# Expert gate/up weights read as one run per partition in a DeltaNet, attention and MoE layer

## The reference, cut to what matters

```python
def moe_ffn(x, router_w, router_bias, w_gate_up, w_down, ws_gate_up, ws_down):
    scores = sigmoid(xt @ router_w)                      # 512 x 64
    _, sel = lax.top_k(scores + router_bias, TOP_K)
    ...
    gu = x_pad[tok] @ w_gate_up[e]                       # w_gate_up[e]: 1024 x 512
    h = jax.nn.silu(gu[:, :EXPERT_DIM]) * gu[:, EXPERT_DIM:]
    y = (h @ w_down[e]) * wt[:, None]                    # w_down[e]: 256 x 1024
    ...
x = layer_norm(ALPHA * x + mix, ln1_g[l], ln1_b[l])
x = layer_norm(ALPHA * x + ffn, ln2_g[l], ln2_b[l])
```

## Time and profile before

| | |
|---|---|
| runs of the kernel before, median (lowest, highest) | 1773.01 us (1768.64, 1789.97) |
| the profiled execution: span from first to last instruction | 1775.4 us |
| busy: TensorE, VectorE, ScalarE, GpSimd | 82%, 29%, 18%, 18% |
| mean granted TensorE clock | 0.885 of full speed |
| SyncE's DMA queue | 167040 packets, 268.85 MB |
| GpSimd's DMA queue | 11008 packets, 25.45 MB |
| store of one tile to x1_rows, issue to landing | 2.6 us |
| expert stage, final stage in the trace | about 1070 to 1690 us, 1705 to 1775 us |

### The profile page before, as it was taken

The page is one execution under the profiler, slowest core; times in us unless marked ns, Lnnn a source line. Parts: engine busy times, 40 slices in busy tenths (PEclk is TensorE's granted clock), DMA queues, the critical chain, the costliest instruction groups (busy, mean ns, idle before and its releaser), DMA issues. The chain is left out here.

```text
span 1775.4 us, 21709 instructions
## 1 busy us (share of the span) xinstructions
PE 1455.1 (82%) x7304; PEld 864.8 (49%) x7305; DVE 518.1 (29%) x932; ACT 325.1 (18%) x848; POOL 311.8 (18%) x379
## 2 busy tenths in 40 slices
PE   7999999999998998799996938898869868985900
PEld 5566556655663332588745524454444434443400
DVE  1544444444431233233331831111101101110127
ACT  1231333133221223222201000111101101110100
POOL 1202220221121111100012011122112212221113
PEclk8999999999998887799997859999879978997955
DMA  3611111111000000343404507899999996899653
GB/s 98 179 36 35 35 35 35 33 28 33 0 0 24 24 24 0 84 112 95 159 24 175 210 28 253 293 340 398 396 394 348 397 397 244 306 398 396 234 221 142
DMA packets 178919, 295.93 MB, mean 167 GB/s; under 512 B 11504, under 2 KB 81232, under 8 KB 178880
## 3 DMA queue, kind: packets, MB, share of 16 engines
q1 hardware_dynamic: 167040, 268.85, 42.8%
q0 software_dynamic: 11008, 25.45, 3.8%
q10 hardware_dynamic: 832, 1.11, 0.2%
HBM read 284.86 MB, written 22.83 MB: 173 GB/s over the span
## 5 line engine op out<-in xcount | busy, mean ns | idle before, releaser
L1686 PE MATMUL bank<-expert_gu,gathered_xT 128*64 128x256 f32 x2048 | 254.7, 405 | 47.9 <-DMA expert_gu<-in_expert_w_gate_up_dram 36.2
L402 PE MATMUL bank<-xT,w_head 128*128 128x512 f32 x480 | 239.7, 606 | 0.8 <-PEq L77 0.8
L1686 PEld LDWEIGHTS bank<-expert_gu,gathered_xT 128*64 128x64 f32 x2048 | 161.5, 146 | 129.1 <-DMA expert_gu<-in_expert_w_gate_up_dram 38.1
L1827 DVE SCALAR_TENSOR_TENSOR hidden<-gate,slot_w,bank 128x128 f32<-128x128 f32 x64 | 22.2, 348 | 412.5 <-ACT gate L1798 412.5
L568 POOL TENSOR_TENSOR LO<-LT,masks 128x512 f32<-128x512 f32 x56 | 69.4, 1266 | 372.3 <-DVE LT L723 372.3
L1693 PE MATMUL bank<-expert_down,hiddenT 128*64 128x512 f32 x512 | 125.0, 609 | 0.6 <-issue 0.6
L402 PEld LDWEIGHTS bank<-xT,w_head 128*128 128x128 f32 x480 | 81.2, 197 | 41.6 <-issue 41.6
L1798 ACT ACTIVATE gate<-bank 128x128 f32<-128x128 f32 x64 | 17.8, 279 | 353.3 <-PE bank L1686 353.3
L1615 POOL DMA_INDIRECT y_rows<-expert_y,row_col x64 | 64.4, 1006 | 49.4 <-POOL row_col L1612 47.5
L1134 DVE TENSOR_TENSOR w_lo<-w_tile,w_hi 128x1024 fp32r<-128x1024 f32 (+1 forms) x32 | 36.0, 1127 | 125.3 <-ACT w_hi L1088 125.3
L1612 POOL COPY row_col<-row_idx 128x1 int32 (+1 forms) x64 | 11.7, 183 | 328.2 <-ACT expert_y L1804 327.7
(11 more groups left out here) (353 smaller groups left out, 2259.0 us busy)
## 6 DMA issues: line engine op xcount, KB each, us to landing
expert_gu<-in_expert_w_gate_up_dram SPq DMA_DIRECT2D x64, 2048.0 KB
expert_down<-in_expert_w_down_dram SPq DMA_DIRECT2D x64, 1024.0 KB, 19.9
w_head<-in_w_in_dram SPq DMA_DIRECT2D x32, 512.0 KB, 3.8
choices<-y_rows SPq DMA_DIRECT2D x24, 512.0 KB, 15.1
w_tile<-in_w_in_dram SPq DMA_DIRECT2D x16, 512.0 KB, 4.0
w_tile<-in_w_branch_a_dram SPq DMA_DIRECT2D x8, 512.0 KB, 5.4
w_pair<-in_w_in_dram SPq DMA_DIRECT2D x6, 512.0 KB, 3.8
x_rows<-in_x_dram SPq DMA_DIRECT2D x4, 512.0 KB
```

The costliest lines, as they stand in the source:

```text
L402: mm = nc.tensor.matmul(bank[:, :], w_head[:, g, c, :], xT[:, c, :], start=(c == 0), stop=(c == KC - 1))
L1686: mm = nc.tensor.matmul(bank[parts[a], 0:2 * P], x[:, c, part], halves[:, a, :, :], start=(c == 0), stop=(c == KC - 1))
```

## The change

1. Gate/up weights of an expert: partition p gets model columns 8p to 8p+7, which lie together in DRAM, as one run of 16 KB, instead of eight rows of 2 KB at columns p, 128+p and so on. The router's and the shared expert's gate/up weights are read in the same order (runs of 2 KB and of 16 KB).
2. So that x has the same order, ScalarE writes a permuted copy of each normalised tile (`permute`), and both the store to `x1_rows` and the transposes read it. The copies lie in buffers that the merge no longer uses. SyncE waits for the four stores at the end of the phase.
3. Final stage: eight transfers, each with three choices of a tile (runs of 12 KB). GpSimd adds choices 0 and 1, VectorE adds 2, 3, 4, 5 and then that pair. The bias is added by GpSimd on one half of the columns and by VectorE on the other.

```diff
+    x_cols = [T["av"][:, 2 * t:2 * t + 2, :].rearrange("p a n -> p (a n)") for t in range(2)] + \
+             [w_t[:, KC * t:KC * (t + 1), :].rearrange("p a n -> p (a n)") for t in range(2)]
...
             for t in range(TT):
-                sp.wait_ge(ln_done[t], 1)
-                sp.dma_start(x1_rows[t * P:(t + 1) * P, :], xs[:, t, :]).then_inc(x1_out, 16)
+                sp.wait_ge(permuted[t], 1)
+                sp.dma_start(x1_rows[t * P:(t + 1) * P, :], x_cols[t]).then_inc(x1_out, 16)
+            sp.wait_ge(x1_out, 16 * TT)
...
-                        pe.wait_ge(ln_done[t], 1)
+                        pe.wait_ge(permuted[t], 1)
...
+            def permute(t):
+                act.wait_ge(ln_done[t], 1)
+                nc.scalar.copy(x_cols[t].rearrange("p (c q) -> p c q", c=KC),
+                               xs[:, t, :].rearrange("p (q c) -> p c q", c=KC)).then_inc(permuted[t], 1)
...
                 nc.scalar.activation(mv[:, t, 3:4], mv[:, t, 2:3], ACT.Exp, scale=-0.5).then_inc(ln_rs[t], 1)
+                if t:
+                    permute(t - 1)
+            permute(TT - 1)
...
-            sp.dma_start(wr[:, :, :], router_w.rearrange("(c p) n -> p c n", p=P)).then_inc(r_in, 16)
+            sp.dma_start(wr[:, :, :], router_w.rearrange("(p c) n -> p c n", p=P)).then_inc(r_in, 16)
...
-            sp.dma_start(wg[:, :, :], ws_gu.rearrange("(c p) n -> p c n", p=P)).then_inc(s_in, 16)
+            sp.dma_start(wg[:, :, :], ws_gu.rearrange("(p c) n -> p c n", p=P)).then_inc(s_in, 16)
...
-                for k in (4, 5, 0, 1, 2, 3):
-                    sp.dma_start(yt[:, t, k, :], rows[t, :, k, :]).then_inc(y_in[t][k], 16)
+                for m in range(PARTS):
+                    k = m * TOPK // PARTS
+                    sp.dma_start(yt[:, t, k:k + TOPK // PARTS, :].rearrange("p k c -> p (k c)"),
+                                 rows[t, m, :, :]).then_inc(y_in[t][m], 16)
...
+            def add_bias(t):
+                pool.wait_ge(ln_m[t], 1)
+                at = slice(0, HALF)
+                nc.gpsimd.tensor_tensor(xs[:, t, at], xs[:, t, at], b_row[:, at], ALU.add).then_inc(ln_done[t], 1)
+
             for t in range(TT):
...
+                pool.wait_ge(y_in[t][0], 16)
+                nc.gpsimd.tensor_tensor(yt[:, t, 0, :], yt[:, t, 0, :], yt[:, t, 1, :], ALU.add).then_inc(pair_done[t], 1)
+                if t:
+                    add_bias(t - 1)
+            add_bias(TT - 1)
...
+                dve.wait_ge(ln_m[t], 1)
+                at = slice(HALF, D)
+                nc.vector.tensor_tensor(xs[:, t, at], xs[:, t, at], b_row[:, at], ALU.add).then_inc(ln_done[t], 1)
...
-            part = expert_w_gate_up[0][bass.ds(e, 1)].rearrange("e (c p) n -> p (e c) n", p=P)
+            part = expert_w_gate_up[0][bass.ds(e, 1)].rearrange("e (p c) n -> p (e c n)", p=P)
```

More of the change, by code:

```diff
@@ L987, in merge_phase @@
     x1t_psum, x1t_ready = mem.sem("x1t_psum"), mem.sem("x1t_ready")
+    permuted = mem.sems("permuted", TT)
     xs, xT, dnT, aoT, ident, eps = T["x"], T["xT"], T["dnT"], T["aoT"], T["ident"], T["eps"]
@@ L1005, in merge_phase @@
     TURNS = KC // 2
+    x_cols = [T["av"][:, 2 * t:2 * t + 2, :].rearrange("p a n -> p (a n)") for t in range(2)] +              [w_t[:, KC * t:KC * (t + 1), :].rearrange("p a n -> p (a n)") for t in range(2)]
     def two_on(i, p, k):
@@ L1076, in _ @@
                     if c == 0:
-                        pe.wait_ge(ln_done[t], 1)
+                        pe.wait_ge(permuted[t], 1)
                     if c >= 4:
                         pe.wait_ge(x1t_ready, c - 3)
-                    mm = nc.tensor.transpose(ps[c % 4][:, t * P:(t + 1) * P], xs[:, t, c * P:(c + 1) * P], ident[:, :])
+                    mm = nc.tensor.transpose(ps[c % 4][:, t * P:(t + 1) * P], x_cols[t][:, c * P:(c + 1) * P], ident[:, :])
                 mm.then_inc(x1t_psum, 1)
@@ L1867, in final_phase @@
 def final_phase(nc, mem, T, ps, ln_g, ln_b, y_rows, out):
-    y_in = [mem.sems(f"y_in{t}_", TOPK) for t in range(TT)]
+    PARTS = 2
+    y_in = [mem.sems(f"y_in{t}_", PARTS) for t in range(TT)]
     s_done, pair_done = mem.sems("s_done", TT), mem.sems("pair_done", TT)
@@ L1874, in final_phase @@
     xs, eps = T["x"], T["eps"]
+    HALF = D // 2
     yt = mem.sb("choices", [P, TT, TOPK, D])
@@ L1878, in final_phase @@
     mv = mem.sb("ln2_mv", [P, TT, 4])
-    rows = y_rows.rearrange("(t p k a) c -> t p k (a c)", t=TT, p=P, k=TOPK)
+    rows = y_rows.rearrange("(t p m k a) c -> t m p (k a c)", t=TT, p=P, m=PARTS, k=TOPK // PARTS)
     with nc.Block() as block:
@@ L1885, in _ @@
             for t in range(TT):
-                for k in (4, 5, 0, 1, 2, 3):
-                    sp.dma_start(yt[:, t, k, :], rows[t, :, k, :]).then_inc(y_in[t][k], 16)
+                for m in range(PARTS):
+                    k = m * TOPK // PARTS
+                    sp.dma_start(yt[:, t, k:k + TOPK // PARTS, :].rearrange("p k c -> p (k c)"),
+                                 rows[t, m, :, :]).then_inc(y_in[t][m], 16)
             for t in range(TT):
-                sp.wait_ge(ln_done[t], 1)
+                sp.wait_ge(ln_done[t], 2)
                 sp.dma_start(out[0, t * P:(t + 1) * P, :], xs[:, t, :]).then_inc(out_done[t], 16)
@@ L1906, in _ @@
         def _(pool):
+            def add_bias(t):
+                pool.wait_ge(ln_m[t], 1)
+                at = slice(0, HALF)
+                nc.gpsimd.tensor_tensor(xs[:, t, at], xs[:, t, at], b_row[:, at], ALU.add).then_inc(ln_done[t], 1)
             for t in range(TT):
[L1908 to L1914, removed]
+                pool.wait_ge(y_in[t][0], 16)
[3 more added lines that the diff above has]
+            add_bias(TT - 1)
         @block.vector
         def _(dve):
-            HALF = D // 2
             for t in range(TT):
-                for i, k in enumerate((4, 0, 1, 2, 3)):
-                    dve.wait_ge(*((pair_done[t], 1) if k == 4 else (y_in[t][k], 16)))
+                for i, k in enumerate((2, 3, 4, 5, 0)):
+                    if k == 0:
+                        dve.wait_ge(pair_done[t], 1)
+                    elif k in (2, 3):
+                        dve.wait_ge(y_in[t][k // 3], 16)
                     if i:
@@ L2005, in load_gu @@
         def load_gu(sp, s, e, free=None):
-            part = expert_w_gate_up[0][bass.ds(e, 1)].rearrange("e (c p) n -> p (e c) n", p=P)
+            part = expert_w_gate_up[0][bass.ds(e, 1)].rearrange("e (p c) n -> p (e c n)", p=P)
             if free:
                 free()
-            sp.dma_start(T["wgu"][:, s, :, :], part).then_inc(T["gu_in"][s], 16)
+            sp.dma_start(T["wgu"][:, s, :, :].rearrange("p c n -> p (c n)"), part).then_inc(T["gu_in"][s], 16)
         def load_down(sp, s, e, free=None):
```

## The result

The changed kernel takes 1830.84 us (median of 4 runs, 1827.49 to 1838.57) against 1781.49 us (4 runs, 1768.64 to 1791.19) for the kernel before on the same chip: a ratio of 1.028 [1.0226, 1.0334]. The forecast was 1760 with a range to 1790. The profiled executions span 1831.1 and 1775.4 us.

| profiled execution | to the merge | merge | routing to the first expert product | experts | last stage | span |
|---|---|---|---|---|---|---|
| before | 721.7 | 233.8 | 109.4 | 640.5 | 70.0 | 1775.4 |
| after | 738.9 | 236.1 | 109.7 | 675.1 | 71.4 | 1831.1 |
| after, profiled again | 721.5 | 236.6 | 108.3 | 673.1 | 71.2 | 1810.8 |

What follows compares the result with a forecast made beforehand. Weight transfers were taken to bound 344 us of the expert stage, TensorE and overflow blocks the rest outside, VectorE the last stage. -21 + 5 + 0.6 + 2 = -13 from the 1773.0 us median gave 1760, range 1744 to 1790.

Steps and rivals of the forecast that it cites:

- What longer packets do to the other queue: Expert stage: GpSimd's gathers land 2 us later (bounds 0 and 4.2) behind longer weight packets; 5 us more in all.
- in the full stretches that is free: Expert stage, where DMA is full: later gathers cost nothing, a pair lasting 16.9 us by DMA against 15.2 by the gather.
- Rival B: Expert stage: a gather waits behind a fixed 28 packets, landing after 13.0 us; +44, total 1817, chance 0.09.
- Rival A: Expert stage: each gather packet always waits for a 16 KB one, landing after 11.3 us; +6, total 1779, chance 0.22.
- The weight transfers: Expert stage, full stretches: 16 KB runs make each of 38 gate/up loads 0.55 us shorter; 21 us less (bounds 0 and 33).
- The permutation: Before the experts: ScalarE's last strided copy adds 1.5 us, faster router weight reads give 0.9 back; together +0.6.
- the gain for the router's rows: Router weights read as 2 KB runs instead of 256 B rows: TensorE's bias-row wait 0.9 us less (bounds 0 and 2).
- The last stage: Final adds on VectorE and GpSimd: first tile 3.2 us late, the rest 47.2 instead of 48.6; net +2 (bounds -4 and +6).
- The first meeting: Last stage: VectorE's first add runs beside GpSimd's pair add and takes 3.2 us instead of 1.23, costing 1.95.

Runs made afterwards that it cites:

- e1: The changed kernel with GpSimd issuing a pair's gather before the scatter that stood in front of it: 1765.8 us, ratio 0.989 to the kernel before.
- e12: e1 with a pause before each gather of the loop, GpSimd clearing 4096 columns that nobody reads: 1768.17 us in one execution.
- e2: The kernel before with only the gather issued ahead of the scatter: 1779.28 us, ratio 0.9987 to the kernel before.
- e9: The changed kernel with each scatter cut from 128 rows to 16, the last stage reading the merge's output instead: 1819.89 us in a single execution.
- e4: The changed kernel with each gate/up load cut into four transfers of 4 KB runs: 1772.1 us, ratio 0.9958 to the kernel before.
- e3: The changed kernel with each gate/up load cut into two transfers of 8 KB runs: 1777.07 us, ratio 0.9966 to the kernel before.

## Why the prediction was wrong

**The step that failed** is "What longer packets do to the other queue". It had the place, and bounds of 0 and 4.2 us for what a gather takes longer, and took 2, the middle, for want of a row between the ends. Measured: 5.1 us in the buffer whose landings the trace shows, and about 3.3 in the other (10.4 against 7.1). Without the scatter in front it is 3.0 to 3.3 (10.5 and 10.8 in e1 and e12 against 7.5 in e2), inside the bounds. In the shipped order the scatter has at most 1.1 of it (e9); the bounds left it out. The text also had wrong what an issue waits for: it said the buffer's transposes, but the buffer of the gather issued at 1306.67 was free at 1289.84 already, and the gather stood behind the scatter of 1304.70. From the 2 us followed "in the full stretches that is free", and a term of +5 in the sum, where TensorE's waits for gathers grew by 83.7 us and took the whole gain of the loads with them.

**The threshold made the error large.** The text had the loop: a pair of slots can't be shorter than a gather's landing and the 6.2 us from its transposes to the next issue, so the full stretches stay free up to a landing of 16.9 - 6.2 = 10.7 us. "In the full stretches that is free" should have been read as 1.7 us away from not free. But the 6.2, held fixed, grew too. For the gathers issued from 1268.07 on, up to the issue at 1347.82, the transposes begin 9.9 to 12.5 us after the issue (mean 11.7), and the next issue comes 8.0 to 8.4 us behind them (mean 8.3; 1319.16 to 1327.36 in the timeline above), because the next gather stands behind a scatter that waits for the down products right behind the wait, the slow ones. Together that is 19.9 us a pair, against the 16.9 forecast and 18.0 before. With 8.3 the threshold is at 8.6 us, below the 9 us that the forecast itself gave the gather. The issue-to-need distance in the earlier trace rows, 6.4 us for a gather of 7.0, says it more directly: slack was negative before.

**Rival B** came out by its signs of failure (gathers after 12 us, waits past 40 us). That its number did too (1817 against 1817.4 and 1830.8) is luck: it put 41 us on the expert stage, which grew by 34.6 and 32.6. Its mechanism fails. With runs of 4 KB, 28 packets ahead of 0.16 us each would make 4.3 + 4.5 = 8.8 us, and with 8 KB 10.9; the gather took 7.5 (e4) and 8.5 (e3). The Trainium skill (DMA: Bandwidth & Descriptors, Queues, rings and completion order) has an engine change queues only between packets of some 9 to 17 descriptors. These runs don't decide on it. If a gather's eight rows on an engine are one such packet, they wait once for eight 16 KB runs, an estimated 4.9 us, and that sum is the same as one run in front of each of eight rows. Only eight such waits in a row are excluded, since e1's gather is 3.0 us later in all. Rival A's sum fits best: its 4.2 against 3.0 to 3.3 in e1 and e12, and its 11.3 us for a gather against the 12.2 and 10.4 of the changed kernel. Its waits were too few, since it gave the full stretches 0.6 us a pair.

**The weight transfers** were right in mechanism and size once the gather is out of the way: 410 to 415 GB/s was forecast for the full stretches, 421 measured, and the expert stage is 21.0 us shorter in e1 than in e2 (612.4 against 633.4), the forecast's 21, with some 3 us of chance in it. In the changed kernel none of it shows. Packets fell to the number forecast:

```profile
q1 hardware_dynamic: 105600, 268.85, 39.2%
```

**The permutation** cost more than its +1.5: the strided copy took 2.02 us, not the 1.5 assumed (bounds 1.1 and 4.2), and the gain for the router's rows didn't come, as the wait for the bias row is 7.03 us after 6.81. The merge and the routing together are 2.6 us longer, 1.7 in the second profile, against +0.6. The timeline of the changed kernel, in which the transposes begin 2.1 us after GpSimd's bias add ends:

```profile
963.16 2.34 POOL L1139 TENSOR_TENSOR x_rows<-x_rows,aoT 128x1024 f32<-128x1024 f32 x1 [11.40 <-DVE x_rows L1183]
965.53 2.02 ACT L1096 COPY w_tile<-x_rows 128x1024 f32<-128x1024 f32 x1 [2.60 <-POOL x_rows L1139]
967.61 0.18 PEld L1083 LDWEIGHTS bank<-ident,w_tile 128*128 128x128 f32 x1 [4.44 <-ACT w_tile L1096]
...
980.01 13.91 PE L1285 MATMUL bank<-wr,xT 128*128 128x64 f32 x64 [7.03 <-DMA brow<-in_router_bias_dram]
```

**The last stage** was right: +2 forecast, +1.4 and 1.2 measured. The start of its timeline, engines VectorE and GpSimd:

```profile
1768.06 1.23 DVE L1945 TENSOR_TENSOR x_rows<-x_rows,choices 128x1024 f32<-128x1024 f32 x1 [27.80 <-DMA choices<-y_rows]
1768.11 3.37 POOL L1930 TENSOR_TENSOR choices<-choices 128x1024 f32<-128x1024 f32 x1 [21.38 <-DMA choices<-y_rows]
1772.99 7.16 DVE L1945 TENSOR_TENSOR x_rows<-x_rows,choices 128x1024 f32<-128x1024 f32 x4 [3.70 <-DMA choices<-y_rows]
...
1785.10 9.41 DVE L1945 TENSOR_TENSOR x_rows<-x_rows,choices 128x1024 f32<-128x1024 f32 x5
1786.27 3.32 POOL L1930 TENSOR_TENSOR choices<-choices 128x1024 f32<-128x1024 f32 x1
```

The first data is there 8.3 us after the issue (1759.74), before it was 8.5; the second transfer 4.9 us behind it, forecast 5.1. The first meeting was not VectorE's loss: its add took 1.23 and GpSimd's 3.37, the engine that came 0.05 us later. VectorE lost at the next, and so ended the first tile's adds 3.0 us later than before, counted from the first issue; forecast 3.2. In the second tile its five adds took 9.41 us, 2.9 over the 6.55 of no meeting: a full one and one with a half bias add, forecast 1.95 and 1.0.

**Open.** Why the lateness bends up between 8 and 16 KB (1.4 to 5.1 us), why the two buffers differ, and what a gather of the changed order has in its 4.0 us or more beyond the 3.0 of e1, wasn't settled. Whether a gather waits for one run before each of its rows or once for several stays open too. The split of the stage's 34.6 us into 12.9 of busier products and 21.6 of waiting was read from the profiles, not tested.

## What to carry to other kernels

Before the runs of a large transfer are made longer, list what else uses the same DMA engines and how long each of those has from issue to need. A small transfer that somebody waits for can land later by it (here 7.1 to 12.2 us), and where its slack is already negative every us is lost, with slower products behind the wait on top. Issue such a transfer ahead of anything in its queue that waits for a product; here that one move turned 2.8% slower into 1.1% faster. And take the run only as long as the rate still rises clearly (418 GB/s at 8 KB, 421 at 16 KB here).

## What was not expected of the hardware

- Rate by run length in the full expert stretches, with 4 KB down rows beside it: 396, 410, 418 and 421 GB/s for gate/up runs of 2, 4, 8 and 16 KB (the last in e1).
- The landing of a 128-row gather of 4 KB rows in the stage: 7.1 (kernel before), 7.5, 8.5 and 12.2 us for the same four, at a DMA share of 1.02 to 1.04 for the first three. The scatters of e1 took 8.1 us against 6.2 in e2.
- TensorE's products behind a wait of 6 us took 3.46 us for 1.94, at a granted clock of 0.59 over these 4 us.
- Two elementwise adds that meet on VectorE and GpSimd: the one that starts later loses 1 us or more, whichever engine it is. GpSimd's pair add, 0.05 us behind VectorE's, took 3.37 us; VectorE's add took 2.28 where GpSimd's bias add had begun 0.56 us earlier (alone 2.34 and 1.23).
- ScalarE's copy of 1024 columns read with a stride of 32 bytes: 2.02 us, against 1.055 for a cast of as many contiguous ones.
